# Wider statistics products in the layer norm, and moved ScalarE and VectorE work in a GLA/GDN trunk kernel

## The reference

```python
def layer_norm(x, g, b):
    mu = jnp.mean(xf, -1, keepdims=True)
    var = jnp.mean(jnp.square(xf - mu), -1, keepdims=True)
    return (xf - mu) * lax.rsqrt(var + LN_EPS) * g + b

for i in range(DEPTH):
    x = layer_norm(DEEPNORM_ALPHA * x + FFN_RES * swiglu_ffn(x, ...), ...)
    x = layer_norm(DEEPNORM_ALPHA * x + mixer(x), ...)      # GLA, then GDN
    x = layer_norm(DEEPNORM_ALPHA * x + FFN_RES * swiglu_ffn(x, ...), ...)

# GDN, one chunk of one head (q, k of unit length, conv and silu before)
v_new = u - w @ s
o = (qc * exp(gcum)) @ s + att @ v_new
s = exp(g_last) * s + k_end.T @ v_new
o = rms_norm(o, norm_g) * silu(z)
```

## Time and profile before

| | |
|---|---|
| runs | 3195.50, 3199.63, 3197.17 us, median 3197.17 |
| profiled execution | 3198.44 us, its span 3196.6, mean granted clock 0.982 |
| PE, DVE, ACT, POOL busy | 95%, 42%, 32%, 31% of the span |
| layer norms begin (L427) | 479.5, 839.2, 1323.2, 1807.1, 2684.4, 3167.0 us |
| GDN | 1835 to 2684 us, heads 0 to 3, projection, heads 4 to 7, projection |

### The profile page before, as it was taken

The page is one execution under the profiler, slowest core; times in us unless marked ns, Lnnn a source line. Parts: engine busy times, 40 slices in busy tenths (PEclk is TensorE's granted clock), DMA queues, the critical chain, the costliest instruction groups (busy, mean ns, idle before and its releaser), DMA issues.

```text
span 3196.6 us, 61796 instructions
## 1 busy us (share of the span) xinstructions
PE 3048.8 (95%) x25904; PEld 2915.0 (91%) x25904; DVE 1332.3 (42%) x1923; ACT 1013.1 (32%) x1751; POOL 995.3 (31%) x412
## 2 busy tenths in 40 slices
PE   8999999998999999999999989999999879999997
PEld 8999997887899999899999978888988778999997
DVE  3212253335521313621222667776367655312226
ACT  2111126333341111431211445543344434322112
POOL 3333343221433333433333521111211104333332
PEclk9999999999999999999999999999999989999998
DMA  3222221222122222122222111112112111222222
GB/s 132 73 78 80 74 82 51 81 75 83 60 73 73 79 80 73 63 77 80 73 80 80 60 47 63 69 63 69 61 62 69 63 43 53 80 74 78 80 76 76
DMA packets 62319, 230.62 MB, mean 72 GB/s; under 512 B 8257, under 2 KB 10177, under 8 KB 58754
## 3 DMA queue, kind: packets, MB, share of 16 engines
q1 hardware_dynamic: 56898, 200.27, 19.1%
q10 hardware_dynamic: 5184, 26.74, 2.3%
HBM read 209.76 MB, written 17.22 MB: 71 GB/s over the span
## 4 chain that ended last, share of the span: by engine, by line
PE 70%; issue 21%; POOL 4%; DVE 4%; ACT 1%; POOLq 0%; DVEq 0%; ACTq 0%
PE gem L228 60%; PE gem L582 4%; POOL wl L283 3%; POOL xl L532 1%; PE msc L427 1%; PE gem L418 1%; PE msc L749 1%; PE msc L757 1%; PE msc L448 1%; PE msc L567 0%; DVE work L520 0%; DVE work L948 0%; DVE work L951 0%; PE msc L1194 0%; ACT small L1409 0%
## 5 line engine op out<-in xcount | busy, mean ns | idle before, releaser
L283 POOL TENSOR_TENSOR wl<-raw,wh 128x1024 fp32r<-128x1024 f32 x368 | 932.3, 2534 | 2110.7 <-ACT wh L246 2110.7
L246 ACT CAST wh<-raw 128x1024 fp32r<-128x1024 f32 x368 | 386.5, 1050 | 1425.6 <-PE gem L228 1403.8
L228 PE MATMUL gem<-xh,wh 128*128 128x320 f32 x2688 | 612.7, 309 | 5.0 <-POOL wl L283 5.0
L228 PE MATMUL gem<-xl,wh 128*128 128x320 f32 x2688 | 612.4, 309 | 0.0
L228 PE MATMUL gem<-xh,wl 128*128 128x320 f32 x2688 | 612.3, 309 | 0.0
L228 PEld LDWEIGHTS gem<-xh,wh 128*128 128x128 f32 x2688 | 449.2, 188 | 6.0 <-ACT work L329 5.4
L228 PEld LDWEIGHTS gem<-xh,wl 128*128 128x128 f32 x2688 | 449.4, 188 | 0.0
L228 PEld LDWEIGHTS gem<-xl,wh 128*128 128x128 f32 x2688 | 449.4, 188 | 0.0
L350 DVE TENSOR_TENSOR work<-work,gem 128x640 f32<-128x640 f32 x88 | 72.3, 822 | 878.7 <-PE gem L228 843.3
L228 PE MATMUL gem<-hh,wh 128*128 128x320 f32 x1792 | 409.2, 310 | 2.1 <-issue 2.1
L228 PE MATMUL gem<-hl,wh 128*128 128x320 f32 x1792 | 408.8, 309 | 0.0
(11 more groups left out here) (268 smaller groups left out, 2955.8 us busy)
## 6 DMA issues: line engine op xcount, KB each, us to landing
raw<-wstream SPq DMA_DIRECT2D x368, 512.0 KB, 3.5
work<-gdn_s ACTq DMA_DIRECT2D x8, 1024.0 KB, 5.0
gdn_s_out<-work ACTq DMA_DIRECT2D x8, 1024.0 KB, 4.0
work<-gla_s ACTq DMA_DIRECT2D x4, 1024.0 KB, 6.5
gla_s_out<-work ACTq DMA_DIRECT2D x4, 1024.0 KB, 4.0
x<-x_in SPq DMA_DIRECT2D x2, 1280.0 KB, 8.0
y_out<-x SPq DMA_DIRECT2D x8, 320.0 KB, 2.2
gdn_p_out<-work ACTq DMA_DIRECT2D x8, 128.0 KB, 4.0
```

Source lines behind the costliest of these rows:

```text
L228: mm = pe.matmul(gem[:, par, s, 0:HALF], w, r[:, k, s * HALF:(s + 1) * HALF], start=(k == 0 and n == 0), stop=(k == kts - 1 and n == 2))
L246: act.copy(wh[:, par, :], raw[:, par, :]).then_inc(hi_ready.sem, hi_ready.by)
L283: pool.tensor_tensor(wl[:, par, :], raw[:, par, :], wh[:, par, :].bitcast(F32), ALU.subtract)\
```

## The change

The statistics products write 64 equal columns each (the moving operand is the one column, repeated), and DVE reads the first of every 64; the first group of idle products has 10 for 13. A new helper root_table runs a square root of one column, so that the root's table is loaded where it stands: in a GLA head after the second tile, in a GDN head at its start and after tile 3. In a GDN head conv_end(3) moves from step t = 3 to the end of the head; act_split of tile 4 moves ahead of its Silu; decay_stream(0) moves into step t = 3, and new_stream(0) behind the scaling of the outputs.

```diff
--- before.py
+++ after.py
@@ -412,6 +412,11 @@
         xh_ready = Signal("x_hi_ready", per=KT + 1)
         xl_ready = Signal("x_lo_ready", per=KT)
 
+        WIDE = 64
+
+        def statistic(a):
+            return msc[:, a, 0:TT * WIDE].rearrange("p (t n) -> p t n", n=WIDE)[:, :, 0]
+
         def idle_products(pe, n):
 
             for _ in range(n):
@@ -424,8 +429,8 @@
 
             def means(a, src, first, last):
                 for t in range(TT):
-                    mm = pe.matmul(msc[:, a, t:t + 1], src[:, t * P:(t + 1) * P],
-                                   cs[:, C_MEAN:C_MEAN + 1], start=first and t == 0, stop=last,
+                    mm = pe.matmul(msc[:, a, t * WIDE:(t + 1) * WIDE], src[:, t * P:(t + 1) * P],
+                                   cs[:, C_MEAN:C_MEAN + 1].broadcast_to([P, WIDE]), start=first and t == 0, stop=last,
                                    skip_group_check=True)
                 return mm
             last = (KT - 1) * L + KT - 2
@@ -441,7 +446,7 @@
             mm.then_inc(stat_mm.sem, stat_mm.by)
             pe.wait_ge(rounded.sem, rounded.at(0))
             pe.wait_ge(evacuated[0].sem, evacuated[0].at(half(T)))
-            idle_products(pe, 13)
+            idle_products(pe, 10)
             for j, (b, dg, s) in enumerate(((0, diag_r, 0), (2, diag_n, 0), (0, diag_r, 1), (2, diag_n, 1))):
                 flat = dg.rearrange("p t n -> p (t n)")
                 pe.wait_ge(diag_ready.sem, diag_ready.at(L, j))
@@ -472,12 +477,12 @@
         def dve_ln(dve, ph):
             L = LN_OF[ph]
             dve.wait_ge(mean_mm.sem, mean_mm.at(L))
-            dve.tensor_copy(st[:, 0, 0:TT], msc[:, 0, 0:TT]).then_inc(stat_step.sem, stat_step.by)
+            dve.tensor_copy(st[:, 0, 0:TT], statistic(0)).then_inc(stat_step.sem, stat_step.by)
             dve.wait_ge(stat_step.sem, stat_step.at(L, 0))
             dve.tensor_tensor(tmp5, st[:, 0, 0:TT], st[:, 0, 0:TT], ALU.mult).then_inc(stat_step.sem, stat_step.by)
             dve.wait_ge(stat_step.sem, stat_step.at(L, 1))
             dve.wait_ge(stat_mm.sem, stat_mm.at(L))
-            dve.tensor_tensor(tmp5, msc[:, 1, 0:TT], tmp5, ALU.subtract).then_inc(stat_step.sem, stat_step.by)
+            dve.tensor_tensor(tmp5, statistic(1), tmp5, ALU.subtract).then_inc(stat_step.sem, stat_step.by)
             dve.wait_ge(stat_step.sem, stat_step.at(L, 2))
             eps = LN_EPS * (4.0 if ph[0] == "ffn" else 1.0)
             dve.tensor_scalar(tmp5, tmp5, 0.0, eps, ALU.max, ALU.add).then_inc(stat_step.sem, stat_step.by)
@@ -801,6 +806,10 @@
                 body(i)
             body(GLA_HEADS - 1, last=True)
 
+        def root_table(act):
+
+            act.activation(small[:, 56:57], ones[:, 0:1], ACT.Sqrt)
+
         def act_gla(act, occ):
             b = base["gla", 0]
 
@@ -856,6 +865,7 @@
                 act.wait_ge(gla["ke_mm"].sem, gla["ke_mm"].at(h))
                 act.copy(a_ket, tiles5(pair[0])).then_inc(gla["ke"].sem, gla["ke"].by)
                 tile_out(1)
+                root_table(act)
                 for n in range(NCK):
                     if n % 2:
                         act.wait_ge(gla["o_mm"].sem, gla["o_mm"].at(h, n))
@@ -1389,7 +1399,7 @@
                         freed = (gdn["qk_mm"], s, j) if j < 2 else (gdn["v_mm"], s, j - 2)
                         conv_out(j, s * 4 + (4 + j), freed)
 
-                def tile_out(j):
+                def tile_out(j, split_done=False):
 
                     T = gdn_tile(hf, i, j, last)
                     if j < 4:
@@ -1399,7 +1409,9 @@
                     act.wait_ge(tile_done.sem, tile_done.at(T))
                     act.wait_ge(gdn["att"].sem, gdn["att"].at(s, 1))
                     act.activation(halves(d_z[j - 4]), slot(j % 2), ACT.Silu).then_inc(evacuated[j % 2].sem, evacuated[j % 2].by)
-                    act_split(act, T, j % 2)
+                    if not split_done:
+                        act_split(act, T, j % 2)
+                root_table(act)
                 for j in range(2):
                     act.wait_ge(gdn["qk_mm"].sem, gdn["qk_mm"].at(s, j))
                     for t in range(TT):
@@ -1474,19 +1487,19 @@
                         from_state(t)
                         new_values(t)
                         squares(t - 1)
-                    if t == 3:
-                        conv_end(3)
                 from_state(PT)
                 new_values(PT)
                 squares(3)
                 squares(4)
                 act.wait_ge(gdn["oss"].sem, gdn["oss"].at(s))
                 act.activation(d_ors, d_os, ACT.Sqrt).then_inc(gdn["ostd"].sem, gdn["ostd"].by)
-                tile_out(4)
+                act_split(act, gdn_tile(hf, i, 4, last), 0)
+                tile_out(4, split_done=True)
                 tile_out(5)
                 act.wait_ge(gdn["s_new"].sem, gdn["s_new"].at(s, 1))
                 act.dma_start(gdn_s_out[s], d_sin).then_inc(d_sst.sem, d_sst.by)
                 act.dma_start(gdn_p_out[s], d_s).then_inc(d_sst.sem, d_sst.by)
+                conv_end(3)
             for hf in range(2):
                 gdn_in_line(hf, body)
                 act_projection(act, ("gdn", 0), proj_start(hf), stats=hf == 1)
@@ -1730,6 +1743,7 @@
                         convolve(3, range(2 * t - 2, 2 * t))
                     if t == 3:
                         less_old(PT)
+                        decay_stream(0)
                     dve.wait_ge(gdn["su_mm"].sem, gdn["su_mm"].at(s, t))
                     if t == 0:
                         dve.wait_ge(gdn["s_zero"].sem, gdn["s_zero"].at(s))
@@ -1742,19 +1756,18 @@
                     ins.then_inc(gdn["state"].sem, gdn["state"].by)
                     outputs(t)
                 key_ends(PT)
-                decay_stream(0)
                 decay_stream(1)
                 dve.wait_ge(gdn["vn"].sem, gdn["vn"].at(s, PT))
                 spread_values()
                 outputs(PT)
                 dve.wait_ge(gdn["osq"].sem, gdn["osq"].at(s, NU - 1))
                 dve.tensor_scalar(d_os, d_os, 1.0 / P, RMS_EPS, ALU.mult, ALU.add).then_inc(gdn["oss"].sem, gdn["oss"].by)
-                new_stream(0)
                 dve.wait_ge(gdn["ostd"].sem, gdn["ostd"].at(s))
                 dve.reciprocal(d_ors, d_ors).then_inc(gdn["ors"].sem, gdn["ors"].by)
                 dve.wait_ge(gdn["ors"].sem, gdn["ors"].at(s))
                 flat_o = d_o.rearrange("p t v n -> p (t v) n")
                 dve.tensor_tensor(flat_o, flat_o, bc(d_ors, P), ALU.mult).then_inc(gdn["on"].sem, gdn["on"].by)
+                new_stream(0)
                 new_stream(1)
                 for v in range(2):
                     gate_outputs(v)
```

## The result

The changed kernel takes **3171.3 us** (median of four runs, 3169.5 to 3172.1) against 3196.3 for the kernel before (four runs, 3188.9 to 3199.6); the ratio is 0.9922, 95% interval 0.9904 to 0.9940. The profiled executions differ by 26.8 us in their spans (3196.6 and 3169.8). The forecast was 3175.

The account below looks back on a forecast made before the run. PE has most of the chain, so the end moves only where PE waits at a seam or runs at half clock. Layer norm 11.2 + GDN 10.8 = 22.0 us off the median 3197.2 gives 3175, range 3171 to 3180.

Parts of the forecast that it names:

- The layer norm: Six norms, first statistics product to first whole-tile scaling: 64 columns cost nothing extra and hold the clock; gain 11.2 us.
- The bound of 3.8 us for idle products alone: Layer norm: if the clock falls all the same, only three fewer idle products count, 6 x 0.64 = 3.8 us.
- The turns: From one GDN head to the next: PE's waits shrink by 2.28 us, at five turns and two half ends, 16.0.
- The turn into head 7: GDN turn without tile work as cover: only the shorter way from squares to root counts, 1.03 us.
- The first head of the second half: GDN, start of the second half's first head: gain of about 0.2 us.
- Step (d): GDN head's end: act_split of tile 4 right behind the square root removes PE's 1.09 us wait for POOL at L582.
- Step (c): GDN head's end: new_stream(0) behind the scaling, no load after the last square; swap by itself gains 0.06 us.
- Rival 4: GDN head's end: POOL's earlier split blocks DVE's scaling, losing up to 2.2 us in eight heads, 3192; 2 in 100.
- Step (a): GDN, t = 3: conv_end(3) leaves the step, so PE's L1298, which waited 0.85 us, goes 0.72 earlier.
- The cost at t = 0: GDN: second root_table makes new_values(0) and PE's L1289 0.92 us late in seven heads, 6.4 us lost.
- Rival 1: Head 4's half clock, costing 6.8 us: gone, 3168, 27 in 100; one more head, 3182, 12; five further, 3209, 4.
- The net in GDN: All GDN heads: gains of 17.2 us less the 6.4 us cost, 10.8 us net.

Follow-up runs that it names:

- the best version: The changed kernel with the second root_table of a GDN head moved from ahead of new_values(0) to behind from_state(0); 3163.6 us, ratio 0.9895.

## Why the prediction was right, and where not

**The layer norm, 11.2 us: right**, in mechanism and size. 10.14 us a norm against 10.24 worked out; 64 columns cost what one does; the clock is held. One term inside the sum was off: ten idle products take 1.34 us, not 1.87, and PE then waits 0.44 for DVE's diagonal, so the diagonal sets the time, 0.1 us earlier than said. The gain against the profiled execution of before is 11.9 us. Other executions with the old statistics were dearer than its 72.7: 77.3 us, and 73.8 with ten idle products. So the median of before may hold more half clock in its norms than its profile showed, and part of the 3.7 us by which the kernel beat the forecast may be here; that is not shown, as the timed runs have only a mean clock (below). Another 0.8 is the median of before, which came down from 3197.2 to 3196.3 with its fourth run. The bound of 3.8 us for idle products alone was too wide; it is 2.

**The turns, 16.0 us: right, a little low.** Measured from the last product of t = 3 to the second transposes of v they are worth 2.58, 2.45, 2.57, 2.55 and 2.59 us, and the half ends 2.46 and 2.58: 17.8. By steps: L1308 0.71 (said 0.72), L1325 0.42 more (said 0.41), L1333 nothing more to speak of (said 0.06), L587 1.3 (said 1.09). The turn into head 7 brought 0.8 for 1.03, but not by the load that I named: in the best version without the first root_table the transposes of v stand there 0.2 us later than with it, and most of the rest comes from the earlier L1333. The first head of the second half, put at 0.2, brought nothing.

**Step (d) gave the right sum mostly to the wrong edit.** I put the 1.09 at POOL down to act_split's move. Measured from the last product of t = 3, the run with act_split back has its cast 2.1 us earlier than the kernel before all the same (2034.63 against 2043.51): 1.13 from decay_stream and about 1.0 from the load that no longer stands ahead of the root. PE gets there only 1.1 earlier, so 1.0 of the 1.3 us at L587 comes without the move, and 0.33 with it. That the sum of the turn came out is in this part luck.

**Step (c) overlooked why the order matters.** The swap is worth nothing by itself, as said. Rival 4 named the mechanism that makes it necessary, POOL's split blocking the scaling, with up to 2.2 us; measured, 1.9. It did not occur in the change, because the scaling starts 0.7 us ahead of POOL. The Trainium skill ("GPSIMD Engine Reference", Specifications) has contention for DVE instructions with two SBUF inputs, and the trace agrees: L1770 was blocked, and L1728, whose second input is in PSUM, kept its 1.2 us beside POOL (two in 2.35 us from 2035.18 in the change). DVE's cast, by which the rival says that the trace agrees in kind, has one input only and so is another case: it too was held, 2.55 us in rows 7 and 1.57 at 2040.04 in the change, where it takes 0.49 without POOL. What neither the rival nor that sentence has is the second price, the clock.

**Step (a) overlooked a dependence.** conv_end(3) had to leave t = 3 as soon as the root's table was loaded ahead of it. Taken alone it is worth 0.1 to 0.2 us a turn, too little for the medians; next to the second root_table it is worth 18 us.

**The cost at t = 0, 6.4 us: right.** 0.84 to 0.91 us in the six heads with full clock there, said 0.92. No drain beside the load is seen: the load starts 0.02 behind the end of ACT's cast (2094.70), the dummy root 0.01 behind the load's. The Trainium skill's 1380 ns ("ScalarE: Activation LUTs", What ACT_TABLE_LOAD costs) do not show here. What the prediction didn't say is that the load had a free place one step further on; the change pays 6 us for it, and gains about 8 by the traces; by the medians (3170.1 without the second root_table) the two cancel.

**Rival 1, the half clock in head 4, went for the most part, by chance.** The stretch went from 13.7 to 3.4 us. Head 4's length (from one L1315 to the next, projection included) was 150.3 us with 13.7 us of it and 144.0 in the two kernels with the same GDN code and none: 6.3, where I said 6.8. With the change's code it is 142.1 to 142.8 with none or 3.4 us. It is not tied to the change: stretches of 10 to 14 us stood in this head in four of fourteen profiled executions, those of before, of the best version (145.0) and of two experiments (147.3, 149.3).

**The net in GDN.** 17.8 + 0.8 - 6.1 + 6.3 make 18.8, the profile shows 14.5. The other 4 us went in places that the change doesn't touch: the 3.4 us of half clock left in head 4, 17 us of it at GDN's entry for 13.7, 41 for 38 in head 7, and stops for issue in the small products that move heads by -0.7 to +1.1 us. The timed runs have a mean granted clock on record, but not where it fell: 0.981 at the median of the 58 runs of the kernel before beside the experiments (its profiled execution 0.982), 0.985 to 0.988 in the four of the change (profiled 0.985). The times of those 58 runs follow it closely, from 3189 us at 0.984 to 3209 at 0.978. So both profiles are fair samples, within a few us, but how the 25.1 us divide between the edits and chance stays open to that extent. Without the head-4 accident, the same GDN code took 863.2 and 861.4 us in two executions, the new code 851.4 and 850.3: 11.5 us, for the 10.8 forecast.

## What to carry to other kernels

In the statistics 64 equal columns cost what one column did and kept the clock; with one column, three idle products fewer did not, and brought some 2 us in the norms. A table load goes where its engine waits longest, not where the code has a seam: the same line one step later was worth 7.7 us. And moves made together must be priced together: here two of them brought 2 us and nothing, yet undoing the second without the first cost 20 us, and a third, worth less than 1 us alone, cost 18 when left out beside the new load.

## What the runs showed of the hardware

- DVE's scaling, with two inputs from SBUF, and POOL's split block each other, and the one that comes first runs on. POOL's split, started 0.34 us ahead, made a 1.49 us scaling last 3.41; started 0.73 us behind the scaling (2034.51 against 2033.78), the split took 3.03 for 2.40 instead, which fits a start at the scaling's end. Each is so in all eight heads (3.31 to 3.41, 3.02 to 3.04). DVE's cast with one input is held as well (1.57 to 2.57 us for 0.49); its addition with one input in PSUM is not (1.2).
- A wait on TensorE can be paid twice. Behind waits of 2.3 to 2.4 us the clock went to 0.50, mostly for 3.4 us, six times out of eight in one kernel (new_stream(0) back) and five out of seven in another (conv_end(3) back). With the waits of the change at the same places, none to 0.56 us, it never did, and neither behind the eight waits of 1.6 us at L1325 with decay_stream(0) back.
- Half clock costs nothing where another engine sets the pace: behind norms 2 and 3 it stood for 3.4 us in the change and not at all in the layer norm's part alone, and from there to the next norm both took 471.2 us.
- The same instructions, those of the old norm, spent 3.4, 6.8 or 10.2 us at half clock in one execution or another (11.4, 12.8 or 14.4 us a norm). A single profile of such a stretch is a sample: a forecast should take the spread, not the one value.
